# Token tiles instead of column blocks at the border between the first output projection and the dense feed-forward

## What is computed

```
def sublayer(x, shift, scale, gate, g_pre, g_post, fn):
    h = rmsnorm(x, g_pre) * (1 + scale[:, None]) + shift[:, None]
    out, aux = fn(h)
    return x + gate[:, None] * rmsnorm(out, g_post), aux
```

```
def swiglu(x, w1, w3, w2):
    return (jax.nn.silu(x @ w1) * (x @ w3)) @ w2
```

## Time and profile before

| | us |
|---|---|
| median of 3 runs | 1452.35 |
| lowest, highest | 1451.47, 1454.2 |
| profiled execution | 1452.35 |
| its span | 1450.7 |
| TensorE busy | 1359.2 (94%) |
| VectorE busy | 872.1 (60%) |
| ScalarE busy | 738.5 (51%) |
| chain that ended last, share on TensorE | 76% |

### The profile page before, as it was taken

How to read it: one execution, slowest core, us unless ns; L and a number is a source line. 1 busy time by engine, 2 the same in 40 slices (tenths; PEclk the granted TensorE clock), 3 DMA queues, 4 the chain that set the end, 5 groups by cost and what they waited for, 6 DMA issues and landing times.

```text
span 1450.7 us, 18579 instructions
## 1 busy us (share of the span) xinstructions
PE 1359.2 (94%) x7178; PEld 1068.7 (74%) x7178; DVE 872.1 (60%) x1168; ACT 738.5 (51%) x961; POOL 96.5 (7%) x170
## 2 busy tenths in 40 slices
PE   7999789899999998999989899999999998899996
PEld 3997347799998877987567676657877733688884
DVE  2534676533334436788775695556966603979796
ACT  3432466622233336596264485445865403768674
POOL 0402420000000000200000200000000000000001
PEclk8999999999999999999989999999999999999998
DMA  9943997533443323423862698668998799999993
GB/s 353 294 142 119 362 371 280 204 117 117 134 151 122 117 87 116 134 70 116 313 224 108 248 369 295 235 216 289 404 324 287 270 393 409 410 381 407 377 381 131
DMA packets 132235, 358.17 MB, mean 247 GB/s; under 512 B 6236, under 2 KB 30200, under 8 KB 132024
## 3 DMA queue, kind: packets, MB, share of 16 engines
q1 hardware_dynamic: 120440, 321.53, 60.5%
q0 software_dynamic: 9344, 32.26, 6.4%
q10 hardware_dynamic: 2368, 3.23, 0.6%
HBM read 335.35 MB, written 22.55 MB: 247 GB/s over the span
## 4 chain that ended last, share of the span: by engine, by line
PE 76%; DVE 10%; DMA 6%; ACT 4%; issue 2%; POOL 2%; SPq 1%; POOLq 0%; DVEq 0%; ACTq 0%
PE bank L2306 30%; PE bank L1958 12%; PE bank L1713 7%; PE bank L1969 6%; PE bank L2254 6%; PE bank L1763 4%; PE bank L1710 3%; DMA ring<-in_moe_w_dram 2%; DMA arena<-shear 1%; DMA arena<-in_moe_w_dram 1%; PE bank L1688 1%; PE bank L2194 1%; DMA ring<-in_mod_w_dram 1%; DVE arena L2763 1%; DVE ring_parts L2461 1%
## 5 line engine op out<-in xcount | busy, mean ns | idle before, releaser
L2306 PE MATMUL bank<-arena_parts 128*128 128x512 f32 x1072 | 263.7, 392 | 4.5 <-ACT arena_parts L1457 2.7
L3003 DVE TENSOR_TENSOR ring_parts<-ring,arena_parts 128x2048 fp32r<-128x2048 f32 x85 | 192.4, 2285 | 79.5 <-PE bank L2254 43.9
L2306 PEld LDWEIGHTS bank<-arena_parts 128*128 128x128 f32 x1072 | 199.4, 188 | 54.3 <-issue 11.7
L1457 ACT ACTIVATE arena_parts<-ring 128x2048 fp32r<-128x2048 f32 x85 | 161.3, 1917 | 25.6 <-DMA ring<-in_moe_w_dram 19.5
L2306 PE MATMUL bank<-ring_parts,arena_parts 128*128 128x512 f32 x504 | 136.1, 392 | 2.9 <-DVE ring_parts L3003 2.8
L1958 PE MATMUL bank<-ht_parts,arena_parts 128*128 128x384 f32 x352 | 118.1, 336 | 0.4 <-DVE xn_parts L2472 0.3
L1958 PE MATMUL bank<-ht_parts,ring_parts 128*128 128x384 f32 x352 | 117.6, 334 | 0.0
L1958 PE MATMUL bank<-xn_parts,arena_parts 128*128 128x384 f32 x352 | 117.6, 334 | 0.0
L2306 PEld LDWEIGHTS bank<-ring_parts,arena_parts 128*128 128x128 f32 x504 | 94.9, 189 | 24.0 <-DVE ring_parts L3003 4.2
L2698 DVE TENSOR_TENSOR arena<-arena,bank 128x384 f32<-128x384 f32 x22 | 12.2, 554 | 123.7 <-PE bank L1958 123.7
L1713 PE MATMUL bank<-ht_parts,ring_parts 128*128 128x384 f32 x256 | 85.7, 335 | 0.0
(11 more groups left out here) (501 smaller groups left out, 2646.5 us busy)
## 6 DMA issues: line engine op xcount, KB each, us to landing
ring<-in_moe_w_dram SPq DMA_DIRECT2D x144, 1024.0 KB, 7.0
ring<-in_mod_w_dram SPq DMA_DIRECT2D x24, 2048.0 KB, 12.1
arena<-in_moe_w_dram SPq DMA_DIRECT2D x48, 1024.0 KB, 6.8
ring<-in_ff_w_dram SPq DMA_DIRECT2D x23, 1024.0 KB, 7.8
ring<-in_w_in_odd_dram SPq DMA_DIRECT2D x6, 2048.0 KB, 8.6
ring<-in_w_in_even_dram SPq DMA_DIRECT2D x5, 2048.0 KB, 9.6
ring<-in_ff_w_dram SPq DMA_DIRECT2D x5, 2048.0 KB, 8.1
routed<-cst POOLq DMA_DIRECT2D x1, 7168.0 KB, 23.3
```

The costliest lines, as they stand in the source:

```text
L1457: act.activation(whi_moe[high_at(w, n_)], e_half(j, h), ACT.Copy).then_inc(whi_ready, 1)
L2306: ins = pe.matmul(bank[base + b][:, :], lhs[:, c_, :], rhs[:, k, 512 * b:512 * b + 512], start=(first and h == 0 and k == 0 and n_ == 0), ...
L3003: dve.tensor_tensor(e_half(j, h, low=True), e_half(j, h), whi_moe[high_at(w, 2 * j + h)], ALU.subtract).then_inc(wlo_ready, 1)
```

## The change

At the first border the work goes by token tiles:

- TensorE turns tile 0 in the middle of tile 1's projection (before its second half) and tile 1 in the middle of tile 2's (after 30 of its 48 products), eight transposes each (`turn_tile`), into the two banks that the tile's own product had. The first step of the up-projection runs its 48 products on tokens 0 to 255, then comes `turn_tile(2)`, `gate_row(1, 0)`, and the same 48 products on tile 2's 128 tokens.
- ScalarE modulates a tile behind its norm (`modulate_tile`, eight activations of 128 tokens in place of two per column block), and VectorE splits it (`tile_halves`, four column blocks in one instruction).
- In all three borders each half of a tile signals alone. The two engines don't cross over any more: ScalarE squares a half when it is there, then VectorE multiplies it. The down-projection runs its last four steps half by half for that.
- The gate row of this border goes to banks 0 and 1. Counts of semaphores follow (`NORMED`, `OUT_BASE`).

```diff
             def norm_tiles(s):
+                if s == 0:
+                    for t in range(NT):
+                        root_of_product(0, t)
+                        root_of_sum(0, t)
+                        modulate_tile(t)
+                    return
...
             def root_of_product(s, t):
-                if s == 1:
-                    act.wait_ge(*((tile_done, t + 1) if t < 2 else (f_used, KF)))
-                else:
-                    act.wait_ge(out_done, OUT_BASE[s] + t + 1)
+                act.wait_ge(*half_of_product(s, t, 0))
...
-                act.wait_ge(gated, 3 * s + t + 1)
-                then(act.activation(junk[:, 512:1024], bank[2 * t + 1][:, :], ACT.Square, accum_out=b_))
+                act.wait_ge(*half_of_product(s, t, 1))
+                act.activation(junk[:, 512:1024], bank[2 * t + 1][:, :], ACT.Square, accum_out=b_).then_inc(sq2_ready, 1)
+                act.wait_ge(sq2_ready, 6 * s + 2 * t + 2)
...
+            def modulate_tile(t):
+                c_ = min(t, 1)
+                if t == 0:
+                    act.wait_ge(shifts_ready, 3)
+                for b in range(2):
+                    act.wait_ge(xn_turned, tile_part(1, t, b))
+                    for k in range(4 * b, 4 * b + 4):
+                        ins = act.activation(xnk[:, k, t, :], bank[2 * t + b][:, P * (k % 4):P * (k % 4) + P], ACT.Identity,
+                                             scale=acol[:, 1, k, c_:c_ + 1], bias=modc[:, 0, 24 + k, c_:c_ + 1])
+                    ins.then_inc(v_ready, 1)
...
+            def turn_tile(t):
+                pe.wait_ge(xn_ready, 3 + t + 1)
+                for b in range(2):
+                    for k in range(4 * b, 4 * b + 4):
+                        ins = pe.transpose(bank[2 * t + b][:, P * (k % 4):P * (k % 4) + P], xnk[:, k, t, :], ident)
+                    ins.then_inc(xn_turned, 1)
...
+                        if m == 0 and (t, 4 * j + n) in ((1, 4), (2, 5)):
+                            turn_tile(t - 1)
...
-                ins.then_inc(out_done, 1)
+                    ins.then_inc(out_done, 1)
...
+            pe.wait_ge(gb_kept, 2)
+            panel(("up", 0))
+            for g in range(2):
+                up(0, g, 0, 2 * P)
+            turn_tile(2)
+            pe.wait_ge(v_ready, tile_part(1, 0, 1))
             gate_row(1, 0)
-            for k in range(KD):
-                turn_in(1, k)
-            pe.wait_ge(gb_kept, 3)
             for f in range(KF):
...
+                    up(f, g, 0 if f else 2 * P, T).then_inc((gate_done, up_done)[g], 1)
...
             for t in range(NT):
-                for f in range(KF - F_RING, KF):
-                    ins = down(f, t)
-                if t < 2:
-                    ins.then_inc(tile_done, 1)
+                for n_ in range(2):
+                    for f in range(KF - F_RING, KF):
+                        ins = down(f, t, (n_,))
+                    if 2 * t + n_ < 5:
+                        ins.then_inc(tile_done, 1)
...
+            def tile_halves(t):
+                for b in range(2):
+                    dve.wait_ge(v_ready, tile_part(1, t, b))
+                    part = xnk[:, 4 * b:4 * b + 4, t, :]
+                    high, low = (h_[:, 4 * b:4 * b + 4, P * t:P * t + P] for h_ in (hth, htl))
+                    then(dve.tensor_copy(high, part))
+                    dve.tensor_tensor(low, part, high, ALU.subtract).then_inc(hl_ready, 1)
```

More of the change, by code:

```diff
@@ L1665, in turn_in @@
                     pe.wait_ge(xn_ready, 3 * (s + 1))
[L1666 to L1668 removed]
+                if k >= 4 and s < 3:
+                    pe.wait_ge(v_ready, NORMED[s] + k - 3)
                     if s == 0 and k == 6:
@@ L2687, in _ @@
             norm_tiles(0)
-            for k in range(KD):
-                halves_of(1, k)
             split_up(1)
```

95 lines of the change are left out of this document (51 added, 44 removed).

## The result

The changed kernel takes **1455.77 us** (median of 22 runs, 1451.55 to 1463.19), the kernel before 1451.24 (22 runs on the same chips, 1446.67 to 1457.29): **1.0035 times as long**, 95% interval 1.0022 to 1.0047. The forecast was 1457.2 (1455.4 to 1461.8), slower by more than 0.2%. The measured difference is 4.5 us, 3.2 to 6.8 by the interval. The profiled execution of the changed kernel took 1460.09, 4.3 more than its median, so its span mustn't be set against the span of before without care.

A forecast was written before the change was run, and what follows sets the result against it. TensorE, busy 94% of the span, was taken as the bound, so only its waits could give time back. +6.3 - 0.9 - 0.55 = +4.85 on a span of 1450.7, plus 1.65 to the median, gave 1457.2 us (range 1455.4 to 1461.8).

The forecast's parts named there:

- rival C: First border: TensorE stays at full clock after the 7.3 us wait, total 1455.3 us; chance 0.08.
- The wait before tile 0's turning: In tile 1's projection, TensorE stands 7.3 us for tile 0's normed row, from 248.2 to 255.5.
- Rival D: First border: tile 0's row is ready by 248.2, so the early wait is empty, total 1448.0 us; chance 0.06.
- The clock: After the wait for tile 0, TensorE resumes at half clock for 4 us; bounds 3.4 and 5 us.
- Tile 1 and tile 2 complete, no wait at the second turning: Projection: tile 1 complete at 263.7, its row ready at 269.1 before TensorE's 270.5, tile 2 complete at 275.5.
- Narrow products: Up-projection's first step: products of 256 tokens start 0.12 us apart, those of 128 tokens 0.11.
- Rival A: Up-projection's first step: 128-token products cost two passes, 0.21 us each, 3.2 us more, total 1460.4 us; chance 0.32.
- B: First border: 256-token products take two passes too, or the panel lands late; total 1462 us or more; chance 0.09.
- The tail on ScalarE: Before step 1: gate copies 1.1, panel split 3.7, table 1.3, silu 0.5, altogether 6.6 us, silu read at 291.6.
- the estimate of 1458.6: Total if the skill page's drain of about 1.38 us per table switch lengthened ScalarE's tail by 1.4 us.
- Step 1: Up-projection's step 1, whose start is the yardstick: released by ScalarE's silu at 291.6 instead of 285.3, +6.3 us.
- The other borders: Halves signalling alone shorten TensorE's wait by 0.9 us at the second border and 0.55 at the third.

The follow-up runs named there:

- e6: The changed kernel with the first weight panel's split moved behind tile 0's normed row on ScalarE and VectorE; 1452.78 us, ratio 0.9993.
- e7: The changed kernel with tile 0's and 1's norms ahead of their modulations, both tiles turned later, first SiLU before the second panel's split; 1445.39 us, ratio 0.9957.
- e8: The changed kernel with halves no longer signalling alone, so ScalarE waits for a tile's whole product at all borders; 1459.22 us, ratio 1.0046.
- e2: The changed kernel with tile 0 turned 18 products later and tile 1 behind the whole projection; 1456.45 us, ratio 1.0026.
- e11: The kernel before with unread products in two TensorE waits, 4 ahead of the down-projection, 6 at the second border's turning; 1448.74 us, ratio 0.9966.
- e3: The changed kernel with seven products that nobody reads in the wait before the first turning; 1455.15 us, ratio 1.0013.

## Why the prediction was right, step by step

The forecast 1457.2 stands against 1455.77, +4.85 against +4.5. The time alone doesn't tell it from rival C, 1455.3, nor does the interval; the trace does, with the clock at 0.50 behind the wait. Of the rivals none came. Step by step:

- **The wait before tile 0's turning**, the step that carries the sign: 7.3 forecast, 7.10 measured, released by VectorE's normed row. The reading of the two queues was right: the split stood ahead of the square, and with the split behind the row (e6) 4.3 of the 7.10 are gone. The other 2.8 are tile 0's own chain behind the gate copies, and e7 is rid of them because it also turns later. Rival D named step 1 at 39.8 by the yardstick if the row were ready by 248.2; e7 gave 38.89, but by another way, and that the figures lie close is in part luck. Its figure that the change pays from a wait under 4.3 us on, if the clock stays up, was put to the test by e6 only in part: at a wait of 2.78 with the clock down the kernel was at 0.9993, no gain that can be told.
- **The clock** was mis-sized and hid a scatter. I took it to return 4 us after TensorE resumed; it was 2.8 here (259.0), and the cost 1.5 us (0.8 in the turning, 0.7 in the products) in place of 1.9. But e8 had 5.1 us after the same wait, and 2.5 us of cost. The bounds 3.4 to 5, from two rows, were too narrow at both ends. The term was also counted from the wrong point: in the kernel before, the clock was at 0.50 from 268.6 to 275.4 and from 562.1 to 568.9, 6.8 us both times, as in the changed kernel. The price depends on how much of that falls behind the end of the wait.
- **Tile 1 and tile 2 complete, no wait at the second turning**: right. Tile 2 was complete at 275.75, which is 275.0 on the clock of before, against 275.5: the 0.5 is the clock and the wait.
- **Narrow products**: 0.12 and 0.11 apart, as taken. Rival A (0.21 at 128 tokens) and B fell. The 81 ns of the Trainium skill, page "TensorE: Matmul & The Clock Gate", section "Back-to-back issue gap", don't fit either: for these split products at 128 columns the trace gives 0.11, near the 0.11 between two weight loads in the earlier trace rows.
- **The tail on ScalarE**: gate copies, split, table, SiLU took 284.89 to 291.41, 6.5 us (6.6 forecast), and the SiLU released step 1. The table load is followed by the SiLU after 1.29 us, so the drain of about 1.38 us that the Trainium skill, page "ScalarE: Activation LUTs", section "What ACT_TABLE_LOAD costs", adds to a switch isn't there in these rows, and the estimate of 1458.6 falls with it.
- **Step 1**: +5.4 by the yardstick instead of +6.3. Of the 0.9, some 0.5 is the clock and the wait, 0.4 the stretch from tile 2's completion to the SiLU's read (15.7 for 16.1).
- **The other borders**: -0.9 and -0.6 (-0.9 and -0.55 forecast).
- **The sum** was then 1 us too high on what the change does (4.85 against 3.9), and the median came in between, at +4.5. That two totals agree to 0.3 us where single steps were off by 0.4 to 0.9 is luck. The chance of 0.85 for slower was fair. What no step of it held is that a stall also decides whether the clock falls: 1.4 to 3 us at a time, as large as the terms that I did compute, and it falls alike in places that the change doesn't touch.

## What to carry to other kernels

Before work is moved forward on the engine that sets the pace, read the *other* engines' queues at that moment: an early consumer in an in-order stream turns a harmless lateness into a stall of everything behind it. The remedy was to reorder the producers and to place the consumer behind the moment at which they can deliver (e7: 10 us under the changed kernel by the order of a few lines); either alone gave a fraction of it (e6, e2). Price a wait of TensorE with its clock: each wait here was worth its length plus nothing to 3 us, so a chain that is shortened by 1 us can give less than 1 or, where the clock then stays up, several. A short wait can cost more clock than a long one (3.0 us at a wait of 2.78, 1.4 at 7.10), since less of the time at half clock is spent waiting. Where the wait can't be removed, products that nobody reads, ended just before the awaited event, keep the clock and cost nothing (e11: 5 us for ten products).

## What the runs showed of the hardware

- What the clock costs behind a stall isn't given by the stall's length: TensorE resumed at 0.50 and was back at 1.00 after 2.8 us (wait of 7.10), 5.1 us (again 7.10, e8) and 6.0 us (2.78, e6). The whole stretches at 0.50, which begin in the wait, were 6.8, 10.2 and 6.8 us long. A wait of 0.89 was followed by 0.50 in three profiles (e6, e3, e2) and by 1.00 in two (after, e8); one of 3.60 by 1.00 in two of eleven. Where it fell there, it cost 1.6 to 2.9 us.
- Split products of 256 and 128 tokens start 0.12 and 0.11 apart at full clock, those of 512 0.227: below 256 columns narrowing saves almost nothing.
- Two kernels with the same border (the changed one and e8, both with 7.10 us of wait) differ by 1.05 us at tile 1's turning through the clock alone, so a single profile can't rank edits of 1 us.
